# A four-layer block with product-key experts: norms in pieces, modulation weights one part later, lookups begun from the first token block

## The chip, the cores and the metric

The kernel runs on one core of one Trainium2 chip. The metric is the device time of one execution in microseconds, the median of three runs. The engines are named as the profile names them: PE is TensorE (PEld its weight loads), DVE VectorE, ACT ScalarE, POOL GpSimd, SP SyncE. All arithmetic is in float32.

## What is computed

256 tokens of 1024 features pass four layers. Each layer is: a modulated RMS norm, a mixer, a gated residual, a second modulated norm, a feed-forward part, a gated residual. Shift, scale and gate of each layer come from one vector times a 1024 x 6144 matrix (24 pieces of 1 MB per layer).

```python
mod = c_act @ w_ada + b_ada                      # sh1, sc1, g1, sh2, sc2, g2
h = rms_norm(x, norm1_g) * (1 + sc1) + sh1
x = x + g1 * mixer(h)
h2 = rms_norm(x, norm2_g) * (1 + sc2) + sh2
x = x + g2 * ffn(h2)
```

Layers 0 and 1 mix with sliding-window attention, a short convolution and spatial gating; their feed-forward part is a lookup: for each token and each of 8 heads, two sets of 128 key scores, the best 16 of each, the best 16 of their 256 sums, and for these 16 experts a row of `peer_down` (dotted with the token, Gelu, times a softmax gate) and a row of `peer_up` (weighted and summed). Layer 2 mixes with gated linear attention, layer 3 with a linear recurrence; their feed-forward part is a mixture of 16 experts, two per token. A last norm ends the block.

## The kernel before

**Memory and stages.** Activations lie feature-major (`xT`, `hT`: 128 partitions x 8 feature blocks x 256 tokens). Weights stream in slots of 1 MB through a ring of two (`load`, SP's queue); a slot's buffer is released by the first matmul of the slot behind it. `plan()` gives each stage its stream slots and its PSUM banks, four in rotation (`unit_full`, `unit_taken`). The order on every engine is written out by hand; engines meet at semaphores. An arena of 96 KB a partition is shared by all stages.

**Norm** (`norm`, L611 on PE, L1087 on ACT, L1360 on DVE). ACT waits for the whole residual (`x_ready`), squares in two halves (L1094), PE sums with eight matmuls (L618), DVE adds epsilon (L1363), ACT takes the root (L1096), DVE the reciprocal (L1365), the product over all 2048 columns (L1367) and eight scale-and-shift steps (L1375); then one signal, `h_ready`, lets PE go on.

**Modulation.** The weight pieces land in a ring of seven slots in `wide` (the first seven by SP, the others by POOL in `ada_loads`, each once a slot is read). PE multiplies them into a row per part (`ada_slots`, L634), between the weight slots of the mixers; ACT copies rows (`take_rows`), PE turns them to columns (`mod_cols`, L651), DVE adds the bias and makes gains (`next_mods`). Layer 0's mixer takes in the 40 pieces that are left of layers 0 and 1 (two beside each weight slot), layer 1's the 24 of layer 2 (one beside each), layer 2's the 24 of layer 3, layer 3's none.

**Lookup** (`peer`). PE makes the queries of head h for all 256 tokens (`queries_of`, 16 matmuls of 256 columns), then the key scores of head h (`scores_of`). DVE searches for each of 16 pairs of token block and head (`best`, L1588 on; n = 8 b + h) and writes 16 row numbers (`idx`). POOL fetches 128 rows of 8 KB per number (`gathers`, L489; 1 MB each, 256 a layer) into 14 slots (seven in `wide`, seven in the arena); a slot is used again once PE has weighed its row (`row_done`). DVE makes the dot with the token (`dots_of`, L1669), ACT for groups of four rows the Gelu (L1180), the product with the gate (L1185) and four diagonal matrices (L1192), PE the weighted sum (`weigh`, L781). ACT's exponent for the gate (`gate_of`, L1172) has its place between the takes of queries and scores. At the end ACT copies the sum (L1200), PE transposes it (L608), DVE adds it to `xT` (L1680).

**Mixture** (`moe`). 96 expert pieces of 1 MB and some more for overfull experts pass a ring of 11 slots, seven of them in `wide`, loaded by POOL (`expert_loads`) and SP.

## Time and profile before

| | |
|---|---|
| median of three runs | 2914.43 us (2911.75 to 2922.51) |
| the profiled execution | 2917.51 us, of which the span is 2915.7 us |
| busy: PE, DVE, POOL, ACT | 83%, 41%, 22%, 20% of the span |
| chain that ended last | PE 50%, DMA 28%, DVE 15%, ACT 5% |
| moved | 934 MB, mean 320 GB/s |

The stages in order of time, from the chain and the timelines: layer 0's mixer 43 to 214 us with its output projection from 185, its lookup to 931; layer 1's mixer 946 to 1088, its lookup to 1804; layer 2's mixer 1818 to 2016, its mixture to 2377; layer 3's mixer 2392 to 2533, its mixture to 2897; the last norm and the store. The profile is read in three ways: the page gives busy shares and bandwidth in 40 slices; the chain of waits gives, at each moment, what the end waited for; the timeline of one engine gives each instruction and what ended the idle time before it.

### The profile page before, as it was taken

How to read it: one execution, taken by the hardware profiler on the slowest of the kernel's cores; microseconds unless marked ns; L12 is line 12 of the kernel's file. 1: busy time of each engine (PE TensorE's matmuls, PEld its weight loads, DVE VectorE, ACT ScalarE, POOL GpSimd, SP SyncE). 2: the span in 40 equal slices, each digit the busy share in tenths (PEclk: the TensorE clock that was granted, in tenths of full speed). 3: DMA queues.
4: the chain of work that ended last, by engine and by line, in shares of the span. 5: the costliest groups of instructions: out<-in, count | busy, mean ns of one | idle time of the engine just before them, and what ended most of it. 6: DMA issues, size and time to landing. Idle time of an engine off the chain costs nothing.

```text
span 2915.7 us, 25951 instructions
## 1 busy us (share of the span) xinstructions
PE 2421.9 (83%) x9610; PEld 1279.5 (44%) x9612; DVE 1191.5 (41%) x2851; ACT 585.5 (20%) x1669; POOL 649.2 (22%) x823
## 2 busy tenths in 40 slices
PE   6897987787786987987777786996999988589997
PEld 2466443333332565443333333445454447444543
DVE  1225666667664136567667654023200022330001
ACT  1111332223222021333222222110100012010100
POOL 2102333333332002333333331100122000012200
PEclk8988999999999998999999898997999989799999
DMA  9856999999996656999999996763799113369960
GB/s 382 334 214 250 421 421 422 421 421 422 421 422 280 252 201 255 421 422 421 421 421 421 421 421 286 277 243 130 310 421 421 74 72 116 144 279 421 421 278 15
DMA packets 130077, 934.36 MB, mean 320 GB/s; under 512 B 14240, under 2 KB 16288, under 8 KB 16544
## 3 DMA queue, kind: packets, MB, share of 16 engines
q0 software_dynamic: 114912, 837.01, 69.5%
q1 hardware_dynamic: 15040, 95.70, 8.5%
q8 instruction: 76, 1.25, 0.2%
q14 instruction: 49, 0.40, 0.0%
HBM read 1070.02 MB, written 1.05 MB: 367 GB/s over the span
## 4 chain that ended last, share of the span: by engine, by line
PE 50%; DMA 28%; DVE 15%; ACT 5%; issue 1%; POOL 0%; SPq 0%; DVEq 0%; ACTq 0%
PE units L984 15%; PE units L575 13%; DMA arena<-rows,idx 11%; DMA wide<-rows,idx 10%; PE accs L781 9%; DMA ring<-stream 5%; PE units L962 3%; PE accs L1029 3%; DVE arena L1669 2%; DVE wide L1669 2%; PE accs L634 2%; ACT arena L1192 2%; DMA wide<-ada 2%; PE units L618 1%; DMA wide<-experts 1%
## 5 line engine op out<-in xcount | busy, mean ns | idle before, releaser
L781 PE MATMUL accs<-wide,arena 128*128 128x512 f32 x1036 | 514.0, 651 | 176.0 <-ACT arena L1192 175.8
L781 PE MATMUL accs<-arena 128*128 128x512 f32 x1012 | 482.7, 630 | 99.3 <-ACT arena L1192 99.1
L781 PEld LDWEIGHTS accs<-wide,arena 128*128 128x128 f32 x1036 | 208.9, 207 | 466.4 <-issue 247.2
L575 PE MATMUL units<-arena,ring 128*128 128x256 f32 x1536 | 351.5, 390 | 64.3 <-DVE arena L1856 26.0
L489 POOL DMA_INDIRECT wide<-rows,idx x259 | 244.3, 943 | 604.3 <-PE accs L781 425.8
L984 PE MATMUL units<-wide,arena 128*64 128x512 f32 (+1 forms) x1728 | 369.2, 598 | 9.4 <-DMA wide<-experts 7.7
L781 PEld LDWEIGHTS accs<-arena 128*128 128x128 f32 x1012 | 202.0, 203 | 374.4 <-issue 245.5
L575 PEld LDWEIGHTS units<-arena,ring 128*128 128x128 f32 x1536 | 299.4, 196 | 120.9 <-DVE arena L1375 27.0
L1085 ACT ACTIVATE arena<-units 128x512 f32<-128x512 f32 (+2 forms) x200 | 110.7, 568 | 1110.9 <-PE units L575 466.4
L489 POOL DMA_INDIRECT arena<-rows,idx x253 | 237.8, 940 | 363.8 <-PE accs L781 355.2
L984 PE MATMUL units<-arena 128*64 128x512 f32 (+1 forms) x960 | 232.7, 593 | 0.5 <-ACT arena L1085 0.5
L1669 DVE CUSTOM_DVE_ANT_0 wide<-wide,accs 128x1024 f32<-128x1024 f32 x130 | 156.9, 1219 | 114.0 <-DMA wide<-rows,idx 114.0
L1669 DVE CUSTOM_DVE_ANT_0 wide<-wide,units 128x1024 f32<-128x1024 f32 x129 | 155.8, 1218 | 114.1 <-DMA wide<-rows,idx 114.1
L984 PEld LDWEIGHTS units<-wide,arena 128*64 128x64 f32 (+1 forms) x1728 | 112.3, 126 | 202.7 <-issue 202.0
L1669 DVE CUSTOM_DVE_ANT_0 arena<-arena,units 128x1024 f32<-128x1024 f32 x127 | 153.6, 1219 | 114.7 <-DMA arena<-rows,idx 114.7
L1669 DVE CUSTOM_DVE_ANT_0 arena<-arena,accs 128x1024 f32<-128x1024 f32 x126 | 151.7, 1219 | 102.9 <-DMA arena<-rows,idx 102.7
L1180 ACT ACTIVATE wgt<-dots 128x4 f32<-128x4 f32 x128 | 26.2, 205 | 781.2 <-DVE dots L1669 781.1
L478 POOL DMA_DIRECT2D wide<-experts x123 | 64.8, 529 | 503.8 <-PE units L984 354.8
L575 PE MATMUL units<-ring,arena 128*128 128x512 f32 (+1 forms) x352 | 153.0, 591 | 21.2 <-DVE arena L1375 12.2
L1192 ACT ACTIVATE arena<-ident,wgt 128x128 f32<-128x128 f32 x512 | 161.5, 386 | 0.0
L2039 DVE COPY arena<-units 128x512 f32<-128x512 f32 x44 | 30.4, 692 | 284.4 <-PE units L984 284.4
L2036 DVE TENSOR_TENSOR arena<-arena,units 128x512 f32<-128x512 f32 x22 | 15.1, 687 | 293.4 <-PE units L984 293.4
(298 smaller groups left out, 2027.4 us busy)
## 6 DMA issues: line engine op xcount, KB each, us to landing
wide<-experts POOLq DMA_DIRECT2D x123, 1024.0 KB, 13.4
wide<-experts SPq DMA_DIRECT2D x93, 1024.0 KB
wide<-ada POOLq DMA_DIRECT2D x89, 1024.0 KB, 9.4
ring<-stream SPq DMA_DIRECT2D x70, 1024.0 KB, 6.6
arena<-experts POOLq DMA_DIRECT2D x69, 1024.0 KB, 15.7
arena<-experts SPq DMA_DIRECT2D x51, 1024.0 KB
wide<-ada SPq DMA_DIRECT2D x7, 1024.0 KB, 19.1
wide<-rows,idx POOLq DMA_INDIRECT x259, 21.7
```

The lines of the kernel that those rows point to most:

```text
L478: pool.dma_start(exp_slot(l, i), experts[l - DEPTH, 2 * p + half, s]).then_inc(exp_landed[at], 16)
L489: pool.indirect_dma_start(row_slot(i), None, rows[l], bass.IndirectOffsetOnAxis(ap=idx[:, n, k:k + 1], axis=0)).then_inc(row_landed[i % NS ...
L575: ins = mm(o, a, b, start=start, stop=stop, skip_group_check=True)
L634: ins = mm(ada_bank(l, part)[32 * g:32 * g + 32, :], cact[:, l // DEPTH, k:k + 1].broadcast_to([P, 32]), ada_piece(i)[:, g * 512:(g + 1) * ...
L781: ins = mm(o[:, half * 512:(half + 1) * 512], diag[:, i % (2 * GROUP), :], row_slot(PICKS * l + i)[:, D + half * 512:D + (half + 1) * 512] ...
L962: ins = mm(bank(u)[:, k * P:(k + 1) * P], tok[:, b, (4 * c + k) * P:(4 * c + k + 1) * P], to[:, b, p * P:(p + 1) * P], start=b == 0, stop= ...
L984: ins = mm(o[j * n:(j + 1) * n, :], act[:, j * n:(j + 1) * n], exp_slot(l, i)[:, c * 512:(c + 1) * 512], start=start, stop=stop, skip_grou ...
L1029: ins = mm(acc[d // 2][:, (d % 2) * T:(d % 2 + 1) * T], o[:, d * P:(d + 1) * P], bT, start=False, stop=p == TILES - 1, skip_group_check=True)
L1085: af(o, i, func, **kw).then_inc(unit_taken[u % BANKS], 1)
L1192: ins = af(diag[:, (i + k) % (2 * GROUP), :], ident[:, :], ACT.Copy, scale=s[:, k:k + 1])
L1669: v.tensor_tensor_reduce(out=row, in0=row, in1=h, scale=1.0, scalar=0.0, op0=ALU.mult, op1=ALU.add, accum_out=dots[:, TOPK * n + k:TOPK * ...
L2039: took(v.tensor_copy(o[:, c * 512:(c + 1) * 512], bank(u)[:, :]), u)
```

## The change

**Norms in pieces.** Each residual step signals by itself, ACT squares pairs of feature blocks as they come, PE sums pair by pair. Epsilon goes into the root as its bias; a root of a constant ahead of the norm loads the function table. DVE makes one product per feature block (x times gain times reciprocal), ACT adds the shift per block (Identity with a bias), and PE's next matmuls wait per block. The other roots lose their separate addition in the same way. The result is stored in four parts.

**Modulation one part later.** The eight pieces of part 0 of layer 0 are all loaded by SP. After that each layer's mixer takes in parts 1 and 2 of its own layer and part 0 of the next: 24, 24, 24 and 16 pieces for layers 0 to 3. Columns are made ahead of the output projection. POOL issues the first seven of its pieces ahead of the masks, and the keys behind the last. The expert loads of layer 3 wait until its pieces are read.

**Lookups.** Head 0's queries and scores are made for token block 0 alone, then for block 1. The order of the next queries and scores changes, on ACT too. The last four rows of the last head are weighed one by one, and the sum is copied in halves.

```diff
+def pieces(l):
+    return ((l, 1), (l, 2)) + (((l + 1, 0),) if l + 1 < LAYERS else ())
+def before_of(l):
+    return KT + ADA_SLOTS * l
+def after_of(l):
+    return min(KT + ADA_SLOTS * (l + 1), LAYERS * ADA_SLOTS)
...
+def query_unit(l, h, b=0):
+    return UNIT_OF["pq", l] + ((0, 2)[b] if h == 0 else (3, 6, 7)[h - 1] if h < 4 else 2 * h + 1)
+def keys_unit(l, h, b=0):
+    return UNIT_OF["pq", l] + ((1, 4)[b] if h == 0 else 5 if h == 1 else 2 * h + 4 if h < PH - 1 else 2 * PH + 1)
+def groups(n):
+    return [(0, 4), (4, 4), (8, 4)] + ([(12, 4)] if n < HB - 1 else [(k, 1) for k in range(12, TOPK)])
+def group_count(l, n, g):
+    return (HB * TOPK // GROUP + GROUP - 1) * l + TOPK // GROUP * n + g + 1
...
-            for i in range(ADA_RING):
+            for i in range(ADA_FIRST):
...
+            for s in range(4):
+                sp.wait_ge(h_ready, 2 * LAYERS * KT + 2 * s + 2)
+                sp.dma_start(out.rearrange("(k p) t -> p k t", p=P)[:, 2 * s:2 * s + 2, :],
+                             hT[:, 2 * s:2 * s + 2, :]).then_inc(stored, 16)
+            sp.wait_ge(stored, 16 * 4)
...
-                    if i >= ADA_RING:
-                        pool.wait_ge(ada_read, i - ADA_RING + 1)
+                    pool.wait_ge(ada_read, i - (ADA_RING if i >= ADA_FIRST + ADA_RING else ADA_FIRST) + 1)
...
-                if l == DEPTH:
-                    pool.wait_ge(ada_read, LAYERS * ADA_SLOTS)
+                pool.wait_ge(ada_read, after_of(l))
...
+            ada_loads(ADA_FIRST, ADA_FIRST + ADA_RING)
+            first_masks(0)
+            ada_loads(ADA_FIRST + ADA_RING, after_of(0))
             pool.dma_start(keys_sb[:, :, :], keys[0]).then_inc(keys_landed, 16)
-            first_masks(0)
-            ada_loads(ADA_RING, 2 * ADA_SLOTS)
...
-                if l and l + 1 < LAYERS:
-                    ada_loads(ADA_SLOTS * (l + 1), ADA_SLOTS * (l + 1) + ADA_RING)
+                if l:
+                    ada_loads(before_of(l), before_of(l) + ADA_RING)
...
-                if l and l + 1 < LAYERS:
-                    ada_loads(ADA_SLOTS * (l + 1) + ADA_RING, ADA_SLOTS * (l + 2))
+                if l:
+                    ada_loads(before_of(l) + ADA_RING, after_of(l))
...
+                    if i < len(fresh):
+                        pe.wait_ge(h_ready, fresh[i])
...
-                    if k % (KT // 2) == 0:
-                        pe.wait_ge(sq_ready, 2 * i + 2 * k // KT + 1)
+                    if k % 2 == 0:
+                        pe.wait_ge(sq_ready, 4 * i + k // 2 + 1)
...
+                if l != DEPTH:
+                    mod_cols(UNIT_OF["mods", l], ROWS[l], pieces(l))
...
-                each = 1 if l else 2
-                token_slots(SLOT_OF["q", l], UNIT_OF["q", l], hT, False, each)
+                each = 1
+                token_slots(SLOT_OF["q", l], UNIT_OF["q", l], hT, False, each, h_counts(2 * l))
...
-                spread_over = (6, 6, 4, 4, 4) if l == 0 else (4, 3, 3, 3, 3)
+                spread_over = (4, 3, 3, 3, 3)
...
+            def first_queries(l, b):
+                n, u = SLOT_OF["pq", l], query_unit(l, 0, b)
                 open_bank(u)
-                for b in range(TB):
+                slot_mms(n, [(bank(u)[:, j * P:(j + 1) * P], tile(n, j * KT + k), hT[:, k, b * P:(b + 1) * P],
+                              k == 0, k == KT - 1) for j in range(2) for k in range(KT)],
+                         {15: unit_full[u % BANKS]}, b == 0, () if b else h_counts(2 * l + 1))
...
-                pe.wait_ge(diag_ready, PICKS // GROUP * l + TOPK // GROUP * n + g + 1)
+                pe.wait_ge(diag_ready, group_count(l, n, g))
                 b = n // PH
                 o = accs[:, 0:2 * 512] if b else accs[:, 2 * 512:4 * 512]
-                for k in range(GROUP * g, GROUP * g + GROUP):
+                first, size = groups(n)[g]
+                for k in range(first, first + size):
                     i = TOPK * n + k
+                    last = n % PH == PH - 1 and k == TOPK - 1
                     for half in range(2):
                         ins = mm(o[:, half * 512:(half + 1) * 512], diag[:, i % (2 * GROUP), :],
                                  row_slot(PICKS * l + i)[:, D + half * 512:D + (half + 1) * 512],
-                                 start=n % PH + k == 0, stop=n % PH == PH - 1 and k == TOPK - 1)
+                                 start=n % PH + k == 0, stop=last)
+                        if last and half == 0:
+                            ins.then_inc(half_done, 1)
...
-                queries_of(l, 0)
+                first_queries(l, 0)
+                scores_of(l, 0, (0,))
+                first_queries(l, 1)
                 queries_of(l, 1)
-                scores_of(l, 0)
+                scores_of(l, 0, (1,))
                 for k in range(KT):
                     ins = nc.tensor.transpose(accs[:, k * P:(k + 1) * P], hT[:, k, 0:P], ident[:, :])
                 ins.then_inc(h0_full, 1)
-                for h in (2, 3):
-                    queries_of(l, h)
-                    scores_of(l, h - 1)
+                scores_of(l, 1)
+                queries_of(l, 2)
+                queries_of(l, 3)
+                scores_of(l, 2)
...
+                ada_slots(2)
...
+                ada_slots(2 * KT - 2)
...
-                    act.wait_ge(x_ready, i)
-                else:
+                if i == 0:
+                    act.wait_ge(consts_made, 1)
+                steps.sync()
+                steps(af(st[:, 1, 26:27], eps[:, :], ACT.Sqrt))
+                if i == 0:
                     act.wait_ge(x_landed, 16)
-                for half in range(2):
-                    k = slice(half * (KT // 2), (half + 1) * (KT // 2))
+                for s in range(4):
+                    k = slice(2 * s, 2 * s + 2)
+                    if i:
+                        act.wait_ge(x_ready, pair_count(i, s))
+                    if i % 2:
+                        wait_taken(act, UNIT_OF["out", i // 2] + s)
+                    elif 0 < i <= 2 * DEPTH and s % 2:
+                        wait_taken(act, UNIT_OF["picked", i // 2 - 1] + 2 + s // 2)
                     af(sq[:, k, :], xT[:, k, :], ACT.Square).then_inc(sq_ready, 1)
-                wait_taken(act, UNIT_OF["norm", i])
-                af(rstd[:, :], rstd[:, :], ACT.Sqrt).then_inc(std_ready, 1)
-            def take_rows(at, l, first, end):
-                for part in range(first, end):
+                u = UNIT_OF["norm", i]
+                take(u, rstd[:, :], bank(u)[:, 0:T], ACT.Sqrt, bias=eps[:, :])
+            def shift(i):
+                for k in range(KT):
+                    act.wait_ge(hx_ready, KT * i + k + 1)
+                    sh = (i % 2) * 24 + k
+                    af(hT[:, k, :], hT[:, k, :], ACT.Identity, bias=mods_of[:, i // 2 % 2, sh:sh + 1]).then_inc(
+                        h_ready, 1)
...
+                    first, size = groups(n)[g]
+                    i = TOPK * n + first
+                    act.wait_ge(dot_done, PICKS * l + i + size)
+                    s = wgt[:, g % 2, 0:size]
+                    steps(af(s, dots[:, i:i + size], ACT.Gelu))
                     if g == 0:
                         act.wait_ge(gate_ready, HB * l + n + 1)
                     steps.sync()
-                    for k in range(GROUP):
+                    for k in range(size):
                         steps(af(s[:, k:k + 1], s[:, k:k + 1], ACT.Copy,
-                                 scale=gate[:, n, GROUP * g + k:GROUP * g + k + 1]))
+                                 scale=gate[:, n, first + k:first + k + 1]))
                     if i >= 2 * GROUP or l:
 
-                        act.wait_ge(row_done, PICKS * l + i - GROUP)
-                    for k in range(GROUP):
-                        steps.sync(GROUP - 1)
+                        act.wait_ge(row_done, PICKS * l + i + size - 2 * GROUP)
...
-                    act.wait_ge(row_done, PICKS * l + PICKS // TB * (b + 1))
                     o = accs[:, 0:2 * 512] if b else accs[:, 2 * 512:4 * 512]
-                    af(room(TOP + b * D, D), o, ACT.Copy).then_inc(picked_read, 1)
-                take_queries(0)
+                    for c in range(2):
+                        if c:
+                            act.wait_ge(row_done, PICKS * l + PICKS // TB * (b + 1))
+                        else:
+                            act.wait_ge(half_done, TB * l + b + 1)
+                        af(room(TOP + b * D + 512 * c, 512), o[:, c * 512:(c + 1) * 512], ACT.Copy).then_inc(
+                            picked_read, 1)
+                take_first_queries(0)
+                take_first_scores(0)
+                take_first_queries(1)
                 take_queries(1)
-                take_scores(0)
-                for h in (2, 3):
-                    take_queries(h)
-                    take_scores(h - 1)
+                take_first_scores(1)
+                take_scores(1)
...
+                take_queries(2)
+                take_queries(3)
                 gate_of(0)
+                take_scores(2)
...
+                take_rows(ROWS[l], pieces(l))
...
-                wait_full(dve, u)
-                took(ts(rstd[:, :], bank(u)[:, 0:T], EPS, None, ALU.add), u)
-                dve.wait_ge(std_ready, i + 1)
-                steps(v.reciprocal(rstd[:, :], rstd[:, :]))
-                steps.sync()
-                steps(tt(hT[:, :, :], xT[:, :, :], spread(rstd[:, :], 1, [P, KT, T]), ALU.mult))
-                steps.sync()
                 if i == 0:
                     first_mods()
-                mod, gain = mods_of[:, i // 2 % 2, :], gains_of[:, i // 2 % 2, i % 2, :]
+                wait_taken(dve, u)
+                steps(v.reciprocal(rstd[:, :], rstd[:, :]))
+                steps.sync()
+                gain = gains_of[:, i // 2 % 2, i % 2, :]
                 for k in range(KT):
-                    if i < 2 * LAYERS:
-                        sh = (i % 2) * 24 + k
-                        ins = ts(hT[:, k, :], hT[:, k, :], gain[:, k:k + 1], mod[:, sh:sh + 1],
-                                 ALU.mult, ALU.add)
-                    else:
-                        ins = ts(hT[:, k, :], hT[:, k, :], col("final_g", k), None, ALU.mult)
-                    if k < KT - 1:
-                        steps(ins)
-                ins.then_inc(h_ready, 1)
+                    g = gain[:, k:k + 1] if i < 2 * LAYERS else col("final_g", k)
+                    stt(hT[:, k, :], xT[:, k, :], g, rstd[:, :], ALU.mult, ALU.mult).then_inc(
+                        hx_ready if i < 2 * LAYERS else h_ready, 1)
...
-                            steps(ins)
-                for s in range(4):
-                    wait_taken(dve, UNIT_OF["out", l] + s)
-                v.memset(psr[:, 15:16], 0.0).then_inc(x_ready, 1)
+                            ins.then_inc(x_ready, 1)
...
+                if l != DEPTH:
+                    next_mods(l)
...
-                if l < DEPTH:
-                    next_mods(l)
```

## Rows read from the trace of the kernel before

**Rows 1.** page, bandwidth in 40 slices of the span, GB/s

```profile
GB/s 382 334 214 250 421 421 422 421 421 422 421 422 280 252 201 255 421 422 421 421 421 421 421 421 286 277 243 130 310 421 421 74 72 116 144 279 421 421 278 15
```

**Rows 2.** timeline of GpSimd, 183 to 300 us: start us, us, engine, line, operation [idle <-releaser]

```profile
254.40 1.00 POOL L489 DMA_INDIRECT wide<-rows,idx  x1 [76.12 <-DVE idx L1642]
...
277.12 0.94 POOL L489 DMA_INDIRECT wide<-rows,idx  x1 [5.28 <-PE accs L781]
```

**Rows 3.** chain of waits, 905 to 960 us: start us, us, what

```profile
916.22 1.22 DVE wide L1669
...
919.79 7.15 PE accs L781 x16
...
926.96 1.03 ACT arena L1200
...
928.73 2.17 DVE xT L1680 x8
...
931.11 1.06 ACT arena L1094
...
932.31 5.19 PE units L618 x16
...
938.43 1.76 DVE rstd L1365
...
940.22 3.31 DVE arena L1367
...
946.48 10.05 PE units L575 x16
```

**Rows 4.** chain of waits, 183 to 300 us

```profile
213.43 0.49 DVE xT L1390
...
228.41 15.93 PE units L575 x64
...
245.96 0.48 DVE tv L1596 x2
...
273.23 8.77 PE accs L781 x16
```

**Rows 5.** timelines of VectorE and SyncE's queue, 2886 to 2916 us

```profile
2893.99 3.23 DVE L1405 SCALAR_TENSOR_TENSOR xT<-accs,mods_of,xT 128x256 f32<-128x256 f32 x8 [3.88 <-PE accs L1029]
...
2910.87 0.41 SPq L448 DMA_DIRECT2D out_t<-arena  x1
```

**Rows 6.** groups of instructions, by form: xcount, busy us, mean ns, idle before

```profile
L1085 ACT ACTIVATE arena<-units 128x256 f32<-128x256 f32 x24 | 9.1, 378 | 0.0
...
L634 PE MATMUL accs<-wide,cact 128*32 128x512 f32 x768 | 99.6, 638 | 15.3 <-DMA wide<-ada 15.3
...
L651 PE MATMUL units<-ident,arena 128*128 128x4 f32 x96 | 11.7, 256 | 1.4 <-ACT arena L1103 1.4
```

**Rows 7.** timeline of TensorE, 2440 to 2575 us

```profile
2495.03 8.94 PE L575 MATMUL units<-arena,ring 128*128 128x256 f32 x32 [26.03 <-DVE arena L1856]
...
2505.77 7.14 PE L575 MATMUL units<-arena,ring 128*128 128x256 f32 x32 [1.81 <-DMA ring<-stream]
```

**Rows 8.** timeline of ScalarE, 183 to 300 us

```profile
262.35 1.28 ACT L1172 ACT_TABLE_LOAD   x1
263.64 0.21 ACT L1172 ACTIVATE gate<-gate 128x16 f32<-128x16 f32 x1
```

**Rows 9.** timeline of TensorE, 40 to 190 and 930 to 1062 us

```profile
42.97 9.55 PE L575 MATMUL units<-ring,arena 128*128 128x512 f32 x16 [3.25 <-DVE arena L1375]
...
185.09 5.23 PE L575 MATMUL units<-arena,ring 128*128 128x256 f32 x23
...
1058.63 3.72 PE L575 MATMUL units<-arena,ring 128*128 128x256 f32 x16 [0.59 <-DVE psr L1586]
```

**Rows 10.** timeline of TensorE, 0 to 60 us

```profile
25.16 1.93 PE L634 MATMUL accs<-wide,cact 128*32 128x512 f32 x8 [0.55 <-DMA wide<-ada]
...
34.48 3.46 PE L634 MATMUL accs<-wide,cact 128*32 128x512 f32 x16 [3.03 <-DMA wide<-ada]
```

236 lines of the change are left out of this document (119 added, 117 removed).

## The prediction

> **What bounds the kernel now.** I read the page's bandwidth line first, then the chain of waits around each hand-over between stages, then the timelines of TensorE and GpSimd there. The bandwidth line [rows 1] has 40 slices of 72.9 us. It stands at 421 GB/s through slices 5 to 12 and 17 to 24: these are the expert lookups of layers 0 and 1, and 1 MB there takes 1.05/0.421 = 2.49 us, so the 256 lookups of a layer take 637 us whatever the engines do. They run from the first gather to the last landing, 254.4 to 916.2 us in layer 0 [rows 2, 3]. Between the two plateaus, and between all other stages, the line is low: there the time is a serial hand-over from engine to engine. The reader should see two such seams. From the last residual step to the first best-of search: 213.9 to 246.0 us, 32.0 us [rows 4]. From the last landed row to the first matmul of the next mixer: 916.2 to 946.5 us, 30.3 us [rows 3]. The mixture stages (two stretches near 421 with TensorE as busy) are untouched by the change. So the change is worth what it takes out of the seams, plus 16 MB of modulation weights that leave layer 0's mixer.
>
> **Norm in pieces.** Before, after the last residual step: a memset, two squares of 1.06, eight matmuls 5.19, an addition and a root (0.9, between 937.5 and 938.43), a reciprocal 1.76, a 2048-wide product 3.31, eight scale-and-shift steps up to 946.48 [rows 3]. After: squares follow pair by pair, so one pair (half of 1.06, 0.53) is left behind the last step, and two of eight matmuls behind that (0.9); the addition goes into the root; then reciprocal 1.76, and per feature block one product of 0.40 (eight in 3.23 [rows 5]) and one 256-column ScalarE pass of 0.38 [rows 6], each block released alone. TensorE needs 0.44 per block, so it starts 0.9 us after the reciprocal and isn't starved. The per-block handshakes cost nothing only while DVE's 0.40 is under TensorE's 0.44 (16 in 7.14 [rows 7]); otherwise some 0.1 us a block.
> The shift by Identity is not in the trace. Bounds: no table load (Copy after a root has none) or 1.28 in each of eight norms, 10 us; I take none: the nearest are the copies of queries and scores after the root, and they fit without one (228.41 and 15.93, 0.9 and a copy of 0.6 end at 245.9 [rows 4]).
> The Trainium skill, ScalarE: Activation LUTs, section on table sets, says identity is in every set, which agrees with taking none.
>
> **Start of the lookups, both layers.** Last residual step ends at 213.9 [rows 4]. Square 0.53 to 214.5; TensorE works at the first six matmuls beside this and ends all eight at 216.5; root 217.0; reciprocal 218.8; block 0 at 219.7, block 7 at 222.6. First half of head 0: 16 matmuls of 128 columns at half of 15.93/32 us each, 0.25 (two whole heads in 15.93 [rows 4]), the first eight at the pace of the blocks, the others 2.0 and 1 for a cold clock, 226.0. Take 0.38, two score matmuls 0.5, take 0.38, hops 0.2: best-of starts at 227.5 instead of 246.0. Gain 18.4, and the first gather moves by the same: **-36.8** for two layers.
> Not all of it stays. The query weights (1 MB each) that landed before the first gather now land in the saturated stretch; the order of queries 1 to 3 says 1.3 more pieces, 3.3 us (bounds 0 and 3 pieces, 7.5): **+6.6**.
> New order on ScalarE: the exponent for head 0's gate now stands behind the take of query 3. Before it ran at 263.6 [rows 8], 9.2 after the first gather. Now it runs about 23 after it, DVE stands until then, and the first weighing starts about 31 instead of 18.8 us after the first gather (273.2 - 254.4 [rows 2, 4]). The ring of 14 rows covers 14 x 2.49 + 2 pieces of queries + latency = 42 us; row 15 was issued 22.7 after the first [rows 2] and now about 33. It is covered by 9 us, so I cost it at nothing; with the cover gone each us late is a us of idle DMA.
> The Trainium skill, ScalarE: Activation LUTs, section on what ACT_TABLE_LOAD costs, gives 1283 ns and a drain of 1380 ns behind it. The trace has the load at 262.35 for 1.28 and the exponent at 263.64 [rows 8], no drain, and the trace decides; by the page the gain would be 3 us smaller, by the root table behind the last copy at two lookups' ends.
>
> **End of the lookups and norm 2, 4.** Before, 30.3 us [rows 3]. After: the dot 1.22 as before; one Gelu 0.2, one gate product 0.28, one diagonal 0.39 (a quarter of the groups between 917.5 and 919.8): the row's matmuls begin 2.3 after the landing; each row takes 7.15/4 = 1.79, under 2.49, so the three rows ahead are done. First half ends at 3.2, second at 4.1. Half copies of 0.6, four transposes 0.6, four additions 1.1 (of 2.17 for eight): last x at 7.0. On ScalarE the root table (1.28) loads after the second copy, at 4.7, then four squares of 0.53: 8.6 and not 7.6. Two matmuls 9.5, root 10.0, reciprocal 11.8, first block at TensorE 12.8. 30.3 - 12.8 = 17.5, **-35.0** for two layers (the same work in layer 1).
>
> **Layer 0's mixer.** Before, 42.97 to 185.09, 142.1 us, with two modulation pieces beside each weight slot; layer 1's mixer is the same work with one piece beside each and runs 946.48 to 1058.63, 112.2 [rows 3, 9]. The change gives layer 0 exactly layer 1's load, 24 pieces: -29.9. Added: before the output projection TensorE takes 12 small column matmuls behind a ScalarE copy of the last row, 24 records of 0.12 [rows 6], 2.8, in both layers: **-27.1** for layer 0, and **+2.8** for layer 1. Bounds: none of it hidden (2.8) or all (0).
> At the start eight pieces come by SP's queue and GpSimd's seven next are issued as pieces are read, no longer behind the masks. Alone pieces come every 2.5 us; once GpSimd's queue works beside, the two pieces before the last reads take (34.48 - 25.16)/2 = 4.7 each [rows 10]. Sharing now begins with the first piece read and no longer with the end of the masks. Dropping the keys (1 MB) gives back 2.5; the eighth piece adds 4.7 and the earlier sharing about 3: the last piece is 4.8 later, at 39.2. Behind it the path was 8.5 (to 42.97) and is 6 (the 2048-wide product was hidden here, the reciprocal no longer is). **+2.3**, bounds -4 and +8.
> The Trainium skill, DMA: Bandwidth & Descriptors, section on queues, rings and completion order, says that each DMA engine goes round-robin between queues with work: by that rule early prefetch takes half the rate from the first pieces, which the 4.7 agrees with; were the SP queue served first, the last piece would come at 32 and the sum be 7 lower.
> Layer 1's mixer begins 10 us sooner after its own weights are asked for (5.8 and not 15.4 us after the last x); its constants, keys and seven pieces are 9.7 MB, 23 us: **+2** of slot waits, bounds 0 and 8.
>
> **The other norms.** Norm 5 and 7 (to the router): the last residual step to first block falls by 8.6 as above (228.41 - 219.8 [rows 4]), **-17**. Norm 6 lies behind 3.23 of accumulator steps now overlapped by the squares: -9.8. The last norm: 2897.2 to the store's issue at 2910.87 [rows 5]; now square, two cold matmuls, root, reciprocal end at 2901.5, products 2904.7, and the last of four stores carries a quarter: **-7.3**.
>
> **Layer 3.** 16 pieces are new here. TensorE reads two while DVE convolves and 14 (four products of 0.13 each [rows 6]) in the 26.0 us that it idles before 2495.03 [rows 7]; seven of them must be loaded, 7 x 2.49 + 2 = 19.5, inside the 26. Cover gone, it is a us a us. GpSimd's expert loads queue behind; 11 pieces, 27 us, and until the mixture lie four slots of output projection (28 us), a norm and the routing. Column matmuls 2; the output slots already wait 1.8 for weights [rows 7] and get 1 more: **+3**.
>
> **Sum.** -36.8 + 6.6 - 35.0 - 27.1 + 2.8 + 2.3 + 2 - 17 - 9.8 - 7.3 + 3 = -116.3. The profiled execution took 2917.5 (span 2915.7 and 1.8 around it), the median is 2914.4, 3.1 below: 2917.5 - 116.3 - 3.1 = 2798.
>
> **Rivals.**
> *The ring of rows dries* after the late first weighing. For: 12 us later. Against: 9 us cover. If DVE's catch-up also fails at the second and third group, 10 us per layer are idle: 2818. Chance 0.13.
> *Layer 0's mixer doesn't become layer 1's*, because its ring of two weight slots meets the first pieces' backlog: half of 27 is lost and the start costs 8: 2818. For: 142 against 112 has a cold start in it. Chance 0.13.
> *The moved pieces hold up the experts of layer 3*: the mixture starts with an empty ring, 11 x 2.49 = 27: 2825. It decides if the seven late pieces land more than 40 us late. Chance 0.03.
> *More gain*: waits between queues also go and the backlogs cost nothing: 2785. Chance 0.10.
> *Slower than before.* A row is weighed in 1.79 us and fetched in 2.49. At half the granted clock (the group at 273.2 took 8.77 against 7.15 for the same work [rows 3, 4]) it is weighed in 3.6, and each such row adds 1.1 to the lookups. The later first weighing leaves TensorE idle longer ahead of it. If over 106 of 512 rows were weighed so (116/1.1), the gain is gone, at 150 it is 2963. Before, the plateau of [rows 1] shows none. Chance 0.01.
>
> **How the numbers follow.** Forecast 2798 with chance 0.60, its own range 2785 to 2812 from the bounds above. The range 2776 to 2832 takes in the first four rivals and a bit on either side. A measurement of this kernel tells 0.5%, 14.6 us, from no change: all cases but the last are beyond it; 0.98 faster, 0.01 same, 0.01 slower.
>
> **What would show it.** The first gather 18 us sooner after the last residual step; 13 us from last landing to next mixer; layer 0's mixer at 115; bandwidth still 421 from a few us after the first gather; the expert ring full at the mixture. A low slice inside a plateau, a table load before Identity, or a mixer 0 over 125 us would make the prediction wrong.

## The result and the profile after

The changed kernel takes 2825.6 us (median of four runs, 2823.0 to 2830.5) against 2918.5 of the kernel before in runs on the same chip: a ratio of 0.969, 95% interval 0.966 to 0.972. The forecast was 2798, range 2776 to 2832: faster, and inside the range, but 28 us short of the forecast and outside the likeliest case's own 2785 to 2812. The profiled execution has a span of 2825.0 us, 90.7 less than before, where the sum had said 116.3 less.

The page's bandwidth line, which answers to [rows 1], and its shares of the chain by engine:

```profile
GB/s 327 309 116 379 422 421 422 421 421 421 421 422 309 287 133 358 421 421 422 421 421 422 421 422 310 315 206 134 348 421 421 76 135 195 251 295 421 421 306 16
PE 56%; DMA 25%; DVE 12%; ACT 5%; issue 1%; SPq 0%; DVEq 0%; POOL 0%; ACTq 0%; POOLq 0%
```

The reader should see that both plateaus still stand at 421: what changed are the seams between them. Read seam by seam, with the same two instants in both timelines, the 90.7 us are these (in us, change of the stretch):

| stretch | before | after | change | forecast |
|---|---|---|---|---|
| start to first matmul of mixer 0 | 43.0 | 48.2 | +5.2 | +2.3 |
| mixer 0, to its output projection | 142.1 | 110.9 | -31.2 | -27.1 |
| last residual step to first gather, layers 0, 1 | 40.5, 40.7 | 22.5, 21.8 | -36.9 | -36.8 |
| first gather to last dot, layers 0, 1 | 661.8, 660.7 | 668.8, 668.3 | +14.6 | +6.6 |
| last dot to next mixer, layers 0, 1 | 30.3, 29.3 | 19.5, 17.7 | -22.4 | -35.0 |
| mixer 1 | 112.2 | 115.0 | +2.9 | +4.8 |
| mixer 2 | 162.4 | 166.3 | +3.9 | none |
| output projection 2 to router | 48.8 | 39.5 | -9.3 | -8.5 |
| mixture 2's end to mixer 3 | 18.4 | 8.9 | -9.5 | -9.8 |
| mixer 3 | 103.4 | 108.0 | +4.6 | +2 |
| output projection 3 to router | 50.5 | 45.3 | -5.2 | -7.5 |
| last accumulation to the end | 21.7 | 13.6 | -8.1 | -7.3 |
| output projections 0, 1 and both mixtures | | | +0.7 | 0 |

(The +3 of layer 3 is split here as the forecast's parts were: 2 of column matmuls, 1 of slot waits.) Three rows carry nearly all of the missing 25.6: the ends of the lookups (12.6), the lookups themselves (8.0), mixer 2 (3.9). And 4.9 of the 31.2 of mixer 0 are not the change's: a stretch of matmuls ran at half clock in the profiled execution of before and not in this one (shown below with e5 and e9).

The end of layer 0's lookup in the chain of waits, which answers to [rows 3]; the last dot stands at 880.83 in VectorE's timeline:

```profile
870.98 1.22 DVE arena L1750
...
873.33 1.18 ACT arena L1281 x4
...
874.55 14.02 PE accs L841 x32
...
888.59 0.60 ACT arena L1293
...
889.20 1.15 ACT L1155
...
891.37 3.71 PE units L666 x16
...
895.60 1.76 DVE rstd L1470
...
897.39 2.22 DVE arena L1475
...
900.29 4.85 PE units L619 x6
```

The reader should see that the chain does not pass through the last landed row (880.8) at all: it left the DMA at the twelfth of the last 16 rows (the dot at 870.98; counted from 0, as below, row 11), and from 874.55 TensorE had work without a gap for 14.0 us, eight rows. It ends 7.7 us after the last dot began, not 4.1. The last rows were single; the group ahead of them was not.

The beginning of the same layer's lookup, timeline of GpSimd, beside [rows 2]:

```profile
211.99 1.01 POOL L529 DMA_INDIRECT wide<-rows,idx  x1 [78.11 <-DVE idx L1723]
...
249.53 0.94 POOL L529 DMA_INDIRECT wide<-rows,idx  x1 [20.06 <-PE accs L841]
...
254.71 1.28 POOL L529 DMA_INDIRECT wide<-rows,idx  x1 [0.30 <-PE accs L841]
268.39 0.94 POOL L529 DMA_INDIRECT wide<-rows,idx  x1 [12.40 <-PE accs L841]
```

The 15th gather was issued 37.5 us after the first, and the 19th waited another 12.4. Stretches of 10 us there (us, PE, PEld, DVE, ACT, POOL busy, granted clock, DMA share, GB/s):

```profile
260.00:270.00 10.00, 7.17 (x23) 4.04 (x22) 4.00 (x9) 8.23 (x24) 0.94 (x1) 0.83 0.70 289
270.00:280.00 10.00, 10.00 (x25) 4.40 (x24) 6.37 (x12) 3.56 (x15) 5.40 (x6) 1.00 0.99 364
```

289 and 364 GB/s instead of 421: (132 x 10 + 57 x 10)/421 is 4.5 us of transfer lost in 20 us. The first weighing stood 33.9 us behind the first gather (245.88) where 31 were reckoned. The later part is in TensorE's timeline: a wait of 3.82 us before the matmuls of query 3, whose weights now land among the gathered rows, and matmuls of 9.67 us behind it where 7.07 is usual.

```profile
226.53 9.67 PE L619 MATMUL units<-arena,ring 128*128 128x256 f32 x32 [3.82 <-DMA ring<-stream]
```

### The profile page after: what moved, and what is told of

Read it like the earlier page. It is cut to its first block, busy times and chain, and to the rows that moved or that the text cites. A ratio compares the mean times of both kernels' runs of the same rounds, so it can differ in the third digit from the quotient of the medians.

```text
span 2825.0 us, 26197 instructions
## 1 busy us (share of the span) xinstructions
PE 2418.4 (86%) x9676; PEld 1280.1 (45%) x9676; DVE 1168.9 (41%) x2825; ACT 622.1 (22%) x1774; POOL 645.4 (23%) x823
## 4 chain that ended last, share of the span: by engine, by line
PE 56%; DMA 25%; DVE 12%; ACT 5%; issue 1%; SPq 0%; DVEq 0%; POOL 0%; ACTq 0%; POOLq 0%
PE units L1051 15%; PE units L619 15%; PE accs L841 12%; DMA wide<-rows,idx 10%; DMA arena<-rows,idx 9%; DMA ring<-stream 4%; PE units L1029 3%; PE accs L1096 3%; DVE wide L1750 2%; DVE arena L1750 2%; PE accs L683 2%; ACT arena L1281 2%; DMA arena<-ada 1%; ACT wgt L1274 1%; PE units L666 1%
## 5 line engine op out<-in xcount | busy, mean ns | idle before, releaser
L841 PE MATMUL accs<-arena 128*128 128x512 f32 x1012 | 489.0, 637 | 102.7 <-ACT arena L1281 102.7
L619 PE MATMUL units<-arena,ring 128*128 128x256 f32 (+1 forms) x1600 | 355.5, 384 | 36.8 <-DMA ring<-stream 21.9
L1269 ACT ACTIVATE wgt<-dots 128x4 f32<-128x4 f32 (+1 forms) x134 | 27.4, 205 | 738.1 <-DVE dots L1750 738.0
L504 POOL DMA_DIRECT2D wide<-ada x88 | 46.4, 534 | 474.5 <-PE accs L683 357.8
```

The costliest lines, as they stand in the source:

```text
L504: pool.dma_start(ada_piece(i), ada[i]).then_inc(ada_landed[(i - ADA_FIRST) % ADA_RING], 16)
L619: ins = mm(o, a, b, start=start, stop=stop, skip_group_check=True)
L841: ins = mm(o[:, half * 512:(half + 1) * 512], diag[:, i % (2 * GROUP), :], row_slot(PICKS * l + i)[:, D + half * 512:D + (half + 1) * 512] ...
```

## Experiments

Each of the first four and of e7, e8, e10 to e12 is the changed kernel with one edit or a few; e5 and e6 start from the kernel before. Ratios are to the kernel before on the same chip.

### The ring dries at the second group of rows

ScalarE's order in the lookup:

```diff
+                gate_of(0)
                 take_queries(2)
                 take_queries(3)
-                gate_of(0)
                 take_scores(2)
```

> The changed kernel with one edit in each lookup: ScalarE makes the exponent of head 0's gate ahead of the take of query 2 instead of behind that of query 3. Theory (the ring of 14 rows dries because the first weighing is late): the first weighing starts about 34 us after the first gather in the changed kernel (245.88 against 211.99) and the 15th gather waits 20 us; with the exponent at about 216.5 VectorE makes the dots from 225 on, the first weighing starts about 5 us sooner, the 15th gather too, and from first gather to last landing falls from 668.8 to about 664 us in each layer: 2817 us in all, about 8 less than the changed kernel. Rival (the 7 us more are only the bytes of the query weights and TensorE's own work): first weighing sooner, the length of the lookup unchanged, 2825 us.

2817.8 us, ratio 0.966 (0.965 to 0.968). The timeline of ScalarE of this run, and that of GpSimd:

```profile
220.02 0.21 ACT L1260 ACTIVATE gate<-gate 128x16 f32<-128x16 f32 x1
```

```profile
214.26 1.01 POOL L529 DMA_INDIRECT wide<-rows,idx  x1 [78.19 <-DVE idx L1723]
...
247.70 0.94 POOL L529 DMA_INDIRECT wide<-rows,idx  x1 [15.94 <-PE accs L841]
...
266.14 0.94 POOL L529 DMA_INDIRECT wide<-rows,idx  x1 [12.15 <-PE accs L841]
```

The exponent runs at 220.0 and not at 238.15; the 15th gather comes 33.4 us after the first and not 37.5, the 19th 51.9 and not 56.4. The stretch as long after the first gather as the low one (262 to 272) now moves 421 GB/s, the next one 398. From first gather to last dot: 665.9 and 664.2 us, 2.9 and 4.1 less. This is the theory's effect at nearly its size; the rival (unchanged length) falls. Of the 7.0 and 7.6 us by which the lookups had grown, some 3 to 4 were a dry ring and the rest is what the moved bytes cost, 4.1 and 3.5 against the 3.3 of the sum.

### The end of the lookup: where the backlog comes from

First the third group of the last head two by two.

```diff
-    return [(0, 4), (4, 4), (8, 4)] + ([(12, 4)] if n < HB - 1 else ...)
+    if n < HB - 1:
+        return [(0, 4), (4, 4), (8, 4), (12, 4)]
+    return [(0, 4), (4, 4), (8, 2), (10, 2)] + [(k, 1) for k in range(12, TOPK)]
```

> The changed kernel with the third group of four rows of the last head weighed two by two, so that TensorE starts on the first two of them 5 us sooner. Theory (at the last landing TensorE still has that group's 7.1 us of work ahead of it, because its diagonals come only when all four rows are there): the last matmul of the weighted sum ends about 4 us after the last landing and no longer 7.7, the next mixer starts 3.6 us sooner in each layer, 2818 us. Rival (the last landing is followed by a chain through dot, gate and diagonal that is as long by itself): no change, 2825 us.

2819.6 us, ratio 0.967 (0.965 to 0.968), but the rows don't show the reason given: the weighted sum ends 7.2 and 6.4 us after the last dot began (7.7 in the changed kernel), 0.5 and 1.3 sooner and not 3.6. Timeline of TensorE, layer 0:

```profile
870.05 3.78 PE L843 MATMUL accs<-wide,arena 128*128 128x512 f32 x4 [3.70 <-ACT arena L1283]
873.62 13.05 PE L843 MATMUL accs<-arena 128*128 128x512 f32 x28
886.51 7.03 PE L843 MATMUL accs<-wide,arena 128*128 128x512 f32 x16
```

A row is four records and takes 1.98 us by itself at full clock, 1.76 to 1.86 in an unbroken series; after 3.7 us of waiting the first took 3.78, at a granted clock of 0.50 (870 to 874 us). The eleven rows behind it ran without a gap: the backlog had moved one group forward, to rows 4 to 7. My expectation failed because I counted only the group next to the end.

Then the opposite, the last four rows as one group again (`[(12, 4)]` for every n).

> The changed kernel with the last four rows of the last head weighed as one group again, as in the kernel before. By the prediction's step the one-by-one is worth the weighing of three rows and the waits of four, about 6 us per layer: 2837 us. By the theory of the backlog (the four single rows wait for TensorE, which ends 7.7 us after the last landing; with one group it starts 3.5 after the landing and ends at 10.6) it is worth only 3 us per layer: 2831 us.

2834.0 us, ratio 0.972 (0.971 to 0.974). The sum ends 10.7 us after the last dot began in both layers, as it did before the change [rows 3: 926.9 - 916.2], and the next mixer begins at 22.3 and 20.7, 2.8 and 3.0 later than in the changed kernel. So single rows at the end alone are worth 3 us a layer: the backlog's number. The step of the prediction would have asked for 6. The time itself, 8.4 us above the changed kernel's, lies between the two expectations and doesn't decide.

Last, all 16 rows of the last head one by one.

```diff
+    return [(k, 4) for k in range(0, TOPK, 4)] if n < HB - 1 else [(k, 1) for k in range(TOPK)]
```

> The changed kernel with all 16 rows of the last head weighed one by one instead of the last four only. Two by two for rows 8 to 11 the sum still ended 7.2 and 6.4 us after the last landing, because the group of rows 4 to 7 was late in its turn and its first row was weighed at half clock. Theory (the backlog comes from waiting for four rows, and each such wait also cools the clock): with single rows TensorE keeps step with the landings, 1.8 us of work for each 2.49, the sum ends 4.1 to 4.5 us after the last landing, the next mixer begins 14 to 16 us after it: 3.4 us less in each layer, 2818 us. Rival (ScalarE's handshakes for single rows are too long): the sum ends as late as now or later, 2825 us or more.

2818.7 us, ratio 0.968 (0.965 to 0.972). Timeline of TensorE, the last three rows, the transposes, the norm and the next mixer:

```profile
878.72 1.98 PE L841 MATMUL accs<-wide,arena 128*128 128x512 f32 x4 [0.47 <-ACT arena L1281]
881.18 1.98 PE L841 MATMUL accs<-wide,arena 128*128 128x512 f32 x4 [0.48 <-ACT arena L1281]
883.64 1.98 PE L841 MATMUL accs<-wide,arena 128*128 128x512 f32 x4 [0.48 <-ACT arena L1281]
...
888.44 3.69 PE L666 MATMUL units<-arena,ones 128*128 128x256 f32 x16 [1.47 <-ACT arena L1166]
895.64 1.10 PE L619 MATMUL units<-ring,arena 128*128 128x512 f32 x2 [3.51 <-ACT arena L1176]
```

One row every 2.46 us, 1.98 of work and 0.48 of waiting, at full speed: TensorE follows the landings. The sum ends 4.3 us after the last dot began in both layers (4.1 in the sum of the prediction), the next mixer begins at 14.3 in both, 5.1 and 3.4 sooner. Of the 5.1 in layer 0, 3.4 are the sum and 1.7 belong to the masks of the next section. The theory holds for the sum, and the rival (ScalarE too slow for single rows) falls.

### Root table and masks

```diff
                         weights(n, g)
+                steps.sync()
+                steps(af(st[:, 1, 26:27], eps[:, :], ACT.Sqrt))
                 take_picked(1)
...
-                steps.sync()
-                steps(af(st[:, 1, 26:27], eps[:, :], ACT.Sqrt))
+                if i not in (2, 4):
+                    steps.sync()
+                    steps(af(st[:, 1, 26:27], eps[:, :], ACT.Sqrt))
...
                 if 0 < l < DEPTH:
+                    pool.wait_ge(h_ready, KT * (2 * l + 1))
                     first_masks(l)
```

> The changed kernel with two small edits that act on different rows of the profile. First, ScalarE's root of a constant, which loads the root table at the end of a lookup, stands ahead of the copies of the weighted sum: from the end of the sum to the next mixer 1.2 us less in both layers (11.7 and 10.0 us now). Second, GpSimd's masks of layer 1 wait until the h blocks are made: if VectorE's eight products of norm 2 take 7.04 us (3.26 in the other norms) because GpSimd masks at the same time, they take 3.3 us and the first block is ready 1.7 us sooner; if something else slows them, they stay at 7. Together about 5 us less, 2820 us; the rival for both, no change.

2823.2 us, ratio 0.971 (0.968 to 0.974): too small to tell from the changed kernel by time, so the verdict rests on the rows. VectorE's eight products of norm 2, first in the changed kernel, then here:

```profile
897.39 7.04 DVE L1475 SCALAR_TENSOR_TENSOR arena<-xT,gains_of,rstd 128x256 f32<-128x256 f32 x8
```

```profile
897.00 3.26 DVE L1479 SCALAR_TENSOR_TENSOR arena<-xT,gains_of,rstd 128x256 f32<-128x256 f32 x8
```

In the changed kernel GpSimd's first mask began at 897.38, in the same moment as the products (897.39); here it begins at 900.97, behind them (they end at 900.26). The masks were the cause. From the end of the weighted sum to the next mixer: 9.3 us in both layers, against 11.7 in layer 0 and 10.0 in layer 1. Layer 1 has no masks behind it, so the root's early load is worth 0.7 (expected 1.2; the last additions of VectorE are then what is waited for), and the masks 2.5 - 0.75 = 1.7. The Trainium skill, SBUF — State Buffer, section on who interferes with whom, says that a VectorE instruction with two inputs in SBUF contends with a GpSimd instruction that reads SBUF, and that the one that starts later waits for the other to finish; the first product took 2.22 us where it takes 0.48 alone, and the first mask 1.94, which fits.

Which of the two starts first differs between executions. In the repetition of the unedited changed kernel (e9) the product was ahead, at 901.17, with the mask at 901.34:

```profile
901.17 7.01 DVE L1475 SCALAR_TENSOR_TENSOR arena<-xT,gains_of,rstd 128x256 f32<-128x256 f32 x8
```

The eight products still took 7.01 us together, but the first h block wasn't held up and the mixer began 10.0 us behind the sum, not 11.7; so it was in e1, e2 and e7. The 1.7 us are paid only where the mask is first (the changed kernel's profile, e3, e10). What e8 shows beyond that is in the sum itself: in layer 1 it ended 10.7 us after the last dot began, 3 later than in the changed kernel, because seven rows in a series took 15.32 us there and 12.28 in the changed kernel; the granted clock was 0.50 over their first 4 us (1727 to 1731). A backlog at the end takes up such a loss in full, which is one reason why the time gained so little.

### Layer 0's mixer: bytes or TensorE's work?

Both runs take the kernel before and 16 of its 40 pieces (those with k of 1, 3, 4, 6 in parts 2 to 5).

```diff
-                    pool.dma_start(ada_piece(i), ada[i]).then_inc(ada_landed[i % ADA_RING], 16)
+                    if not skipped(i):
+                        pool.dma_start(ada_piece(i), ada[i]).then_inc(ada_landed[i % ADA_RING], 16)
```

> The kernel before, with 16 of the 40 modulation pieces of layer 0's mixer not fetched; TensorE still multiplies what lies in their slots, so that layer 0's and layer 1's modulation comes out wrong. Theory (layer 0's mixer was long because two pieces beside each weight slot oversubscribe the DMA engines: each weight slot was waited for 8.3 to 9.7 us): without the 16 MB, 40 us of transfer at 0.42 MB a us, the waits go until TensorE's own work is the bound: the mixer takes about 115 us and not 142, the whole 2888 us, about 27 less than before. Rival (it is TensorE's work on the pieces that counts): within 2 us of the kernel before.

```diff
-                    for g in range(4):
+                    for g in range(1 if skipped(i) else 4):
```

> The kernel before, with the same 16 pieces fetched but only a quarter of their matmuls made (the rest of the modulation rows is left incomplete). Theory of the transfers: TensorE waits for the next slot by as much longer, the mixer keeps its 142 us, the whole is within 3 us of the kernel before. Rival (TensorE's work): 16 pieces of three quarters of 0.93 to 1.94 us are 11 to 23 us less, the whole 2892 to 2903 us.

Without the bytes: 2900.6 us, ratio 0.996 (0.994 to 0.999), which is 11 us less (14 by the medians), not 27. Without three quarters of their matmuls: 2908.5, ratio 0.999 (0.997 to 1.001), not clear of noise. The mixer took 125.2 us (43.30 to 168.51) and 133.5 (44.41 to 177.86), against 142.1. Part of both is a thing that changes from run to run. The attention products of this mixer, 48 records, in the kernel before, in the run without the bytes, in the profiled execution of the changed kernel, and in its repetition (e9):

```profile
165.21 10.34 PE L739 MATMUL units<-arena 128*128 128x64 f32 x48
```

```profile
154.51 5.47 PE L746 MATMUL units<-arena 128*128 128x64 f32 x48
```

```profile
142.31 5.75 PE L788 MATMUL units<-arena 128*128 128x64 f32 x48
```

```profile
141.62 10.34 PE L788 MATMUL units<-arena 128*128 128x64 f32 x48
```

The same kernel has them at 5.75 and at 10.34, with a granted clock of 0.92 and 0.64 over 139 to 160 us; ahead of them TensorE had stood 4.75 us for ScalarE in both. e6 has the fast form too (5.47). With 4.9 us taken off, the bytes alone are worth 12 us, the matmuls alone 4, and both together, in the changed kernel (110.9), 26. So neither theory is right by itself. The reading that fits: while the transfers bind, less work for TensorE is filled with waits; once the bytes are gone (idle time of TensorE for DMA in the mixer falls from 10.0 to 3.4 us), the work of 16 pieces at 0.93 us, 15, is what is left to gain, and 14.3 (125.2 to 110.9) is what came, although the changed kernel has 2.8 us of column matmuls in this stretch that e5 hasn't. Both removals together in the kernel before were not run; the 26 is the changed kernel's, which differs in more than the 16 pieces.

### The start, and prefetch that nobody needs yet

```diff
-            ada_loads(ADA_FIRST, ADA_FIRST + ADA_RING)
             first_masks(0)
+            pool.wait_ge(first_landed[ADA_FIRST - 1], 16)
+            ada_loads(ADA_FIRST, ADA_FIRST + ADA_RING)
```

> The changed kernel with GpSimd's first seven modulation pieces held back until the eighth of SP's first pieces has landed, and the masks ahead of them. Theory (from 15 us on the two queues share, so that SP's pieces come every 4.97 us and not every 2.49, and layer 0's mixer afterwards has transfer time to spare, 0.58 to 0.70 of it used between 40 and 120 us): the eighth piece lands at about 32 and not 40 us, the mixer's first matmul is at 40.5 and not 48.2, the mixer itself keeps its 111 us: 2817 us. Rival (the mixer needs the early prefetch): the mixer waits for pieces or weight slots and gives 5 to 8 us back, 2823 to 2826 us.

2821.2 us, ratio 0.967 (0.966 to 0.969). Timelines of TensorE: the eighth piece read and the first matmul of the mixer, in the changed kernel and in this run:

```profile
40.13 1.94 PE L683 MATMUL accs<-arena,cact 128*32 128x512 f32 x8 [3.03 <-DMA arena<-ada]
...
48.16 10.08 PE L619 MATMUL units<-ring,arena 128*128 128x512 f32 x16 [3.51 <-ACT arena L1176]
```

```profile
29.92 1.68 PE L684 MATMUL accs<-arena,cact 128*32 128x512 f32 x8 [1.43 <-DMA arena<-ada]
...
37.67 8.49 PE L620 MATMUL units<-ring,arena 128*128 128x512 f32 x16 [3.51 <-ACT arena L1177]
```

The pieces come 2.48 us apart where they came 4.97 apart, and the mixer begins 10.5 us sooner. Its output projection begins at 158.8 against 159.0: 0.3 us was left in this execution (the median is 4.4 us below the changed kernel's, not the 8 expected). 4.6 us went in two waits for weight slots (2.17 and 2.43), 1.7 in the half-clock matmuls behind the first of them (8.83 where 7.13 is usual), 4.6 in the attention products at half clock. The last is the difference between executions of the section above, so it is not to be charged to the edit; e12 separates the two.

### One part undone, and the version that follows

The changed kernel once more, unedited, for comparison with the next three.

> The changed kernel itself, unedited, on the chip of the three runs below, so that they can be held against it: 2825 us, 0.969 of the kernel before.

2827.4 us (2821.0 to 2831.1), ratio 0.970 (0.968 to 0.972).

```diff
-                return [KT * i + k + 1 for k in range(first, end)]
+                return [KT * i + KT for k in range(first, end)]
```

The routers' first matmuls wait for all eight blocks in the same way.

> The changed kernel with one part undone: TensorE's first matmuls behind each of the norms 0 to 7 wait for all eight h blocks and not block by block. By the prediction's step (VectorE makes a block in 0.40 us, TensorE uses it in 0.44, so that TensorE starts seven blocks sooner and isn't starved) each of the eight norms costs 7 x 0.41 = 2.9 us more: 2848 us, 23 more than the changed kernel. Rival (a matmul that waits for a block runs as late as if it waited for all, or its clock is colder): 2825 to 2835 us.

2850.2 us, ratio 0.978 (0.975 to 0.980), 22.7 more than e9 where 23 were expected. The idle time of TensorE ahead of mixer 0 is 6.30 us against 3.51. Behind layer 0's lookup, where the products run beside the masks, it is worse: 16.3 us from the end of the sum to the mixer, not 11.7 (the mask began first in both). The block-wise hand-over costs no handshake that shows, as the prediction had it.

The next run has the edits of e1, e7 and e8 together, as they are shown above; e12 adds that of e4.

> The changed kernel with the edits that moved their rows, together: the exponent of head 0's gate ahead of the take of query 2 (the two lookups 7 us shorter), the 16 rows of the last head weighed one by one (3.4 us less in each layer), the root table loaded ahead of the copies of the sum (0.7 us less in each) and layer 1's masks behind its h blocks (1.7 us less, once). If they act on different rows and add up: 17 us less than the changed kernel, 2808 us. Rival (the first are hidden by the transfers of the lookup, as layer 0's later start shows the layers drift): half of it, 2817 us.

2807.0 us (2804.5 to 2818.9), ratio 0.965 (0.962 to 0.967), 20.4 less than e9. In the rows: lookups of 666.2 and 664.3 us, 13.75 us from last dot to next mixer in both layers (19.5 and 17.7 in the changed kernel's profile): 16 of the 20 us. Where the rest lies was not followed.

> The same four edits, and GpSimd's first seven modulation pieces held until SP's eight have landed. Alone that edit began layer 0's mixer 10.5 us sooner and got its output projection only 0.4 us sooner: 4.6 us went in waits for weight slots and 5 in a stretch of matmuls at half clock. Theory (the slot waits stay, the half clock does not always come): 0 to 5 us less than with four edits, 2805 us. Rival (the mixer takes all of it back): 2808 us.

2797.6 us (2794.2 to 2801.0), ratio 0.961 (0.959 to 0.963), 29.8 less than e9. The bandwidth line of its page, and its timeline of TensorE:

```profile
GB/s 365 305 125 422 421 421 422 421 421 421 421 422 321 307 92 410 421 421 422 421 421 421 422 421 327 324 166 136 398 420 421 41 137 227 224 318 421 421 300 16
```

```profile
36.92 9.77 PE L621 MATMUL units<-ring,arena 128*128 128x512 f32 x16 [3.50 <-ACT arena L1179]
...
57.56 7.15 PE L621 MATMUL units<-ring,arena 128*128 128x256 f32 x32 [1.82 <-DMA ring<-stream]
...
132.96 6.18 PE L790 MATMUL units<-arena 128*128 128x64 f32 x48
...
150.11 27.87 PE L621 MATMUL units<-arena,ring 128*128 128x256 f32 x128
```

The same places in e11:

```profile
49.93 9.71 PE L620 MATMUL units<-ring,arena 128*128 128x512 f32 x16 [3.51 <-ACT arena L1178]
...
143.96 5.47 PE L789 MATMUL units<-arena 128*128 128x64 f32 x48
...
160.40 29.56 PE L620 MATMUL units<-arena,ring 128*128 128x256 f32 x128
```

The mixer begins at 36.9 and takes 113.2 us, 2.3 more than in the changed kernel: of 11.2 us gained at the start 9 stay. Against e11 it begins 13.0 us sooner and its output projection 10.3 sooner, with the attention products fast in both, and the two spans differ by the same 10.3 (2802.8 and 2792.5). By the medians it is 9.4 us, more than the 0 to 5 expected; e4's profile had made it look worse. Two slot waits stayed (1.82 and 0.17). The intervals of the two ratios just touch (0.959 to 0.963 and 0.962 to 0.967), but each of the five times of e12 (2794.2 to 2801.0) is below each of e11 (2804.5 to 2818.9), so the fifth edit's share is shown by times and rows.

## Why the prediction was right, and where it wasn't

The mechanism, seams taken out and bandwidth unchanged between them, is what the runs show. That the number lies inside 2776 to 2832 is in part luck all the same. The upper part of the range stood for rivals at 2818 and 2825; of the 25.6 us missing in the profile 8.0 are the lookups', most of it the ring of rows that one rival foresaw, and 12.6 come from the end of the lookups, which no rival touched. Mixer 0 meanwhile gave 4.9 us that are not the change's. Of the signs named, two came out against the forecast: 19.5 and 17.7 us, not 13, from last landing to next mixer, and a stretch of low bandwidth at 260 to 280 us. The rival of layer 3's experts didn't occur: its mixture took 349.5 us, 348.4 before.

**Start of the lookups: right.** -36.8 forecast, -36.9 measured (18.0 and 18.9 in the two layers, 18.4 forecast for each). The whole chain of small steps, blocks at 0.4 us, head 0 for token block 0 alone, held within half a microsecond. One term was low: a matmul of 128 columns was taken as half of one of 256, 0.25 us, and a series of 32 took 10.64, 0.33 each.

**End of the lookups: the largest miss, 12.6 us.** The step that failed was "each row takes 1.79, under 2.49, so the three rows ahead are done". It took the last four rows for the whole queue. When the last row landed TensorE was still in the group of rows 8 to 11, whose diagonals had come at 874.5 because they wait for all four of its rows. That is 3.6 us in each layer. e3 shows what four single rows are worth (3 us a layer), e7 what they are worth when the group ahead is single too (4.3 us after the last dot, as forecast). Another 1.7 us, once and in this execution (not in e9), were the masks, and about 1.3 a layer a norm whose last matmuls end 2.3 us behind the last square (1746.1 to 1748.4) and not 0.9: the eight matmuls are a series of 3.69 us, the four squares of 2.17, so TensorE and not ScalarE ends last. The last 1.0 is that layer 1's seam was 29.3 us before and not the 30.3 reckoned with. That the product of norm 2 was exposed to the masks could have been read before: in the kernel before the masks ran at the same place, the 2048-wide product took 3.31 us in layer 0 [rows 3] and 2.29 in layer 1, which is that 1.0, and the third mask 2.57, where it takes 0.64 in e8.

**Lookups: +14.6, not +6.6.** The bytes were right within a microsecond. The late first weighing was costed "at nothing", with 9 us of cover, and the rival "The ring of rows dries" named the mechanism and the place where it would decide, the second group. It happened there: the first refill (15th gather) came 37.5 us after the first and not 33, still in time, but after four rows TensorE makes a query and its scores, and the 19th gather was at 56.4. The 33 was low by its own parts: 22.7 before and 12.2 for the later weighing make 34.9. The rest is that the first weighing stood at 33.9 and not 31, behind TensorE's wait of 3.82 for query 3's weights, a wait that the prediction's bytes did not have. Price 3 to 4 us a layer, not 10. The cover must be counted to the second refill.

**Layer 0's mixer: right by analogy.** 115.0 by the step that took layer 1's 112.2 and 2.8 of column matmuls; 110.9 in the profile and 115.2 in e9, which has the half-clock stretch as the kernel before has it. Like against like it is -26.3 and -26.9, and -27.1 was forecast; the 4 us by which the profile is better are luck. Mixer 1 took +2.9, the column matmuls alone: its slot waits were 2.7 us and 2.5 before, so the +2 for them didn't come. The step did not need to know whether bytes or work bound; had it been reckoned as bytes alone (27 us) or as matmuls alone (11 to 23), e5 and e6 show 12 and 4 in their place, of the 26 that both give together.

**Start: +5.2, bounds -4 and +8.** The last first piece was read at 40.1 (forecast 39.2; its parts, -2.5, 4.7 and 3, make 5.2 and not the 4.8 used, so 39.7). Behind it 8.0 us passed and not 6: the column matmuls at half clock and the chain of additions, reciprocal (1.76), product and shift. The Trainium skill, DMA: Bandwidth & Descriptors, section on queues, rings and completion order, has each DMA engine go round-robin between queues; 4.97 us a piece with two queues and 2.48 with one (e4) agree.

**Table loads: right.** Identity needs none: ScalarE's eight shifts follow the root in every norm with no load between. After the root's own load the next instruction starts at once (889.20 and 1.28, next at 890.50). The Trainium skill, ScalarE: Activation LUTs, section on what ACT_TABLE_LOAD costs, adds a drain of 1380 ns; the trace doesn't agree: of the changed kernel's 88 loads 52 are followed within 0.02 us by the next instruction, and the others by one that waits for another engine. So the price from the rows was the right one.

**Norms 5 to 7 and the last: right**, -9.3, -9.5, -5.2 and -8.1 against -8.5, -9.8, -7.5 and -7.3. The 2.3 missing ahead of the last router are output slots that wait for weights:

```profile
2413.20 3.58 PE L701 MATMUL units<-ident,arena 128*128 128x4 f32 x16 [1.91 <-DVE arena L1936]
...
2427.80 7.14 PE L619 MATMUL units<-arena,ring 128*128 128x256 f32 x32 [2.55 <-DMA ring<-stream]
2438.05 7.14 PE L619 MATMUL units<-arena,ring 128*128 128x256 f32 x32 [3.11 <-DMA ring<-stream]
2447.80 7.14 PE L619 MATMUL units<-arena,ring 128*128 128x256 f32 x32 [2.61 <-DMA ring<-stream]
```

8.3 us in all, against 5.1 before (the 1.81 of [rows 7] and one of 3.27 behind it), with layer 3's expert loads on GpSimd's queue at the same time. The step allowed 1. The 14 pieces were indeed hidden, but for 1.1 us (VectorE is done 104.5 us after the mixer's start, 103.4 before); the column matmuls took 3.6 and not 2. So layer 3 took 8 and not 3: the terms for the column matmuls and for the slot waits were both too small.

**Mixer 2: +3.9, in no step.** 2.5 of it lie from the column matmuls on, where the same records take longer (the small products 3.41 against 1.84 us, the state products 5.65 against 4.98) at a granted clock of 0.70 against 0.76. Whether the change brings that clock or it differs between executions as in mixer 0 was not tried and stays open.

## What to carry to other kernels

When the last items of a stream are made finer, follow the queue back until a landing finds the consumer idle: the group ahead of the fine ones sets the end as long as it waits for its last member. The cover of a ring has to be counted to the second refill, with all that the consumer does between two groups. And a prefetch that shares the DMA engines with the loads somebody waits for makes each of those loads take twice as long there; held back until the needed ones have landed it gave 9 us here, for 2 us of waits later.

## What the runs showed of the hardware

- Two inputs of VectorE in SBUF beside a masking GpSimd: eight products of 128x256 in 7.04 us and not 3.26; moved apart, 3.26 (e8). Whichever started first went through unhindered: the first product took 2.22 us with the mask 0.01 us ahead of it, and the first h block was 1.7 us sooner where the product led by 0.1 to 0.2 us (e1, e2, e7, e9).
- The same 48 small matmuls took 5.5 to 6.2 us in some executions and 10.34 in others; the changed kernel alone had 5.75 and 10.34, with the granted clock at 0.92 and 0.64 over the stretch (2.4 GHz for nearly all of it, or 1.2 for much of it), after the same 4.75 us of standing. It is 5 us of spread that no edit made.
- After a wait of 3.7 us the first row weighed took 3.78 us in e2, 2.78 in e3 and 1.98 in e8: behind the same wait the clock had fallen to half in one execution and not in another. In a rhythm of 1.98 of work and 0.48 of waiting every row took 1.98, at a granted clock of 1.00 (e7).
- Two queues with work halve each other: 4.97 us for 1 MB, 2.48 alone (the changed kernel's start and e4).
- ScalarE's table load took 1.28 us and the next instruction, where it had nothing else to wait for, began within 0.02 us.
